# A mixture-of-experts encoder layer on one core: the router fed from sums before their norm, the last tile's gain and shift moved behind the selector

## The chip, the cores and the metric

The kernel runs on 1 core of one Trainium2 chip. The metric is the device time of that core in microseconds (us), the median of the runs shown. The core has TensorE (PE: matmuls and transposes), VectorE (DVE), ScalarE (ACT), GpSimd (POOL), and SyncE (SP), whose queue starts most transfers. The engines run their own instruction lists in order and wait for each other on semaphores.

## What is computed

One encoder layer on 512 tokens of 1024 values: an input norm, a mixer, a second norm (LayerNorm 1), then the four best of 32 experts for each token, and a last norm. The change lies between the mixer's output projection and the first expert. Cut to what matters there:

```python
mixed = hybrid_mixer(h, ...)                 # ends in y @ w_out + b_out
h = layer_norm(DN_ALPHA * h + mixed, ln1_g, ln1_b)
logits = h @ w_router + b_router             # 512 x 32
top_val, top_idx = lax.top_k(logits, 4)
gates = jax.nn.softmax(top_val, axis=-1)
# every token's row of h goes through its four experts:
#   act = min(glu, 7) * sigmoid(1.702 * glu) * (clip(lin, -7, 7) + 1),  then act @ w_exp_out[e] + b_exp_out[e]
#   weighted with its gate and summed by token
out = layer_norm(DN_ALPHA * h + ff, ln2_g, ln2_b)
```

## The kernel before

**Tiles.** The 512 tokens are four tiles of 128 rows (`x[:, i, :]`, i = 0 to 3), and a matmul covers 128 of the 1024 values at a time (k = 0 to 7). `psum` (named "banks" in the profile) has eight banks of 128x512 float32. The program has two blocks. The first (lines 411 to 1194) holds the mixer, LayerNorm 1, the router and the selection of the first expert's rows; the second (from line 1261) holds the 32 experts and the last norm. Between them all engines meet: none enters the second block before all have left the first.

**The end of the mixer.** `project(i, h, ks)` (L1092) multiplies tile i by half h of the output matrix, eight float32 matmuls of 512 columns. For each tile DVE adds the residual (L867, after four scalings at L859), takes the statistics (L869, L871), ACT takes the root (L635), and DVE normalises (L877), multiplies by the gain (L879) and adds the shift (L881). The result h1 is then used three times: SP writes it to `h1_dram`, from where later experts gather their rows; POOL scales it (L707) and SP writes it to `acc_dram`; and PE transposes it (`turn_h1`, L1128), ACT copies the transpose (`h1T`, L642; it lies in `hT`), and PE multiplies that by the router's weights `w_rt` (`route`, L1137, and one row for the bias, L1138).

**The order on PE** is written out by hand: projections, transposes and routes of neighbouring tiles interleave. After the last projection stand transpose, route and `keep_busy(n)` (L1145), which issues n products of the identity with ones that nobody reads.

**The selector.** Once the logits of all four tiles are there, DVE takes the eight largest of each row (L900), marks the four best as `hot_b` (L917), and PE counts them by expert (L1173, L1176). From the counts DVE gets `cand`, each token's place at each expert (L928), and `sel0` (L935, in `tmp`), a 0/1 matrix that picks the rows of expert 0. PE multiplies h1 by `sel0` (L1191, 32 products): this is expert 0's input, transposed. DVE then makes the gates in three bfloat16 parts (L938 to L945) and the selectors `sel_first` of the first three experts (L935 again); PE multiplies these by token numbers (L1187), and DVE turns the answer into row numbers `dst_row` (L956 to L965). At last DVE takes the low part `x_lo` of the first half of expert 0's input (L967).

**The experts.** A weight chunk of 1 MB sits in one of 12 slots of `raw`. ACT rounds it (`hi`, L1370), DVE takes the rest (`lo`, L1554), and PE makes three passes (L1789): hi by x_hi, lo by x_hi, hi by x_lo. Twelve chunks make one expert. SP loads a chunk as soon as DVE is through with the slot's last content (L1281). Before the first block ends, SP has loaded twelve chunks: eight from about 225 us on, and four once the last projection is done (L435).

## Time and profile before

| what | us |
|---|---|
| median of 3 runs | 1458.41 (1458.26 to 1458.52) |
| the profiled execution, device time | 1458.66 |
| its span, first to last instruction | 1456.9 |
| PE busy in the span | 1421.1 (98%) |
| DVE busy | 1211.8 (83%) |
| ACT busy | 971.5 (67%) |
| last projection ends | 274.1 |
| first product of the first expert | 299.6 |

A row of the trace in order of time gives the start in us, the duration in us (of several merged instructions: from the first start to the last end), the engine, the line of the kernel, the operation, output and inputs with their shapes, and the count. In brackets stands how long the engine had been idle and what ended that. A float32 matmul of the program is two records. A following matmul starts some 0.17 us before the recorded end of the one ahead of it, since matmuls are pipelined; starts are the better measure. The granted clock of TensorE is at its upper level (2.4 GHz, shown as 1.00) nearly all the time (mean 0.995); the lower level, 1.2 GHz, is shown as 0.50.

### The profile page before, as it was taken

The numbers are of one execution on the slowest core, as the hardware profiler recorded it, in microseconds if no ns is written. First come the engines' busy times: TensorE is split into PE (matmuls) and PEld (weight loads), VectorE is DVE, ScalarE is ACT, GpSimd is POOL, SyncE is SP. The second block draws the span as 40 slices with busy tenths as digits, with TensorE's granted clock in tenths as the row PEclk, the third lists the DMA queues.
The fourth block names the chain that finished last, engine by engine and source line by source line (L and its number), as shares of the span: only waits on it lengthen the run. The fifth ranks groups of instructions, "written<-read, shape, count | busy, mean of one in ns | idle before, by whom it ended". The sixth has DMA issues, their size and how long they took to land.

```text
span 1456.9 us, 20291 instructions
## 1 busy us (share of the span) xinstructions
PE 1421.1 (98%) x6459; PEld 1090.5 (75%) x6459; DVE 1211.8 (83%) x1001; ACT 971.5 (67%) x703; POOL 492.1 (34%) x307
## 2 busy tenths in 40 slices
PE   6999989999999999999999999999999999999996
PEld 3466554788888888888888888888888888888873
DVE  5533348589999999999999999999999999999985
ACT  2245660267777777777777777777777777777772
POOL 4200025143333333444444443334333343333101
PEclk9999999999999999999999999999999999999998
DMA  7220227469999999999999999999999999999943
GB/s 262 78 62 29 69 92 277 188 277 382 372 378 377 375 383 381 385 376 387 382 380 387 376 378 385 388 388 380 377 379 380 377 382 377 378 381 377 360 139 129
DMA packets 85733, 459.31 MB, mean 315 GB/s; under 512 B 11848, under 2 KB 26442, under 8 KB 36554
## 3 DMA queue, kind: packets, MB, share of 16 engines
q1 hardware_dynamic: 75190, 431.91, 75.3%
q0 software_dynamic: 9072, 24.39, 7.1%
q10 hardware_dynamic: 1444, 2.66, 0.7%
q8 instruction: 15, 0.25, 0.1%
q14 instruction: 12, 0.10, 0.0%
HBM read 443.92 MB, written 23.66 MB: 321 GB/s over the span
## 4 chain that ended last, share of the span: by engine, by line
PE 78%; DVE 1%; DVEq 0%; issue 0%; ACT 0%; ACTq 0%
PE banks L1789 72%; PE banks L1758 2%; PE banks L1764 2%; PE banks L1825 1%; PE banks L1893 0%; PE banks L1771 0%; PE banks L1898 0%; DVE raw L1723 0%; PE banks L1752 0%; DVE glu_lin L1589 0%; DVE raw L1719 0%; DVEq L1593 0%; ACT hi L1370 0%; DVE glu_lin L1595 0%; ACT raw L1454 0%
## 5 line engine op out<-in xcount | busy, mean ns | idle before, releaser
L1554 DVE TENSOR_TENSOR lo<-raw,hi 128x2048 fp32r<-128x2048 f32 x383 | 863.6, 2288 | 68.5 <-ACT hi L1370 66.7
L1370 ACT ACTIVATE hi<-raw 128x2048 fp32r<-128x2048 f32 x382 | 729.7, 1920 | 243.2 <-PE banks L1789 243.2
L1789 PE MATMUL banks<-hi,x_hi 128*128 128x512 f32 x1040 | 285.3, 396 | 2.8 <-DVE glu_lin L1589 1.5
L1789 PE MATMUL banks<-lo,x_hi 128*128 128x512 f32 x1040 | 279.0, 390 | 0.0
L1789 PE MATMUL banks<-hi,x_lo 128*128 128x512 f32 x1040 | 278.9, 389 | 0.0
L1474 POOL TENSOR_SCALAR sel<-cst,rank_e 128x128 bf16<-128x128 f32 x120 | 211.6, 1775 | 133.5 <-issue 133.5
L1789 PEld LDWEIGHTS banks<-lo,x_hi 128*128 128x128 f32 x1040 | 195.3, 188 | 41.2
L1789 PEld LDWEIGHTS banks<-hi,x_lo 128*128 128x128 f32 x1040 | 195.3, 188 | 41.1
L1789 PEld LDWEIGHTS banks<-hi,x_hi 128*128 128x128 f32 x1040 | 190.4, 188 | 39.8 <-issue 3.5
L1494 POOL DMA_INDIRECT acc_dram<-ye,dst_row x31 | 49.9, 1610 | 363.8 <-ACT ye L1391 363.8
L1789 PE MATMUL banks<-hi,a_hi 128*128 128x512 f32 x496 | 156.3, 396 | 0.0
L1789 PE MATMUL banks<-hi,a_lo 128*128 128x512 f32 x496 | 153.3, 390 | 0.0
L1789 PE MATMUL banks<-lo,a_hi 128*128 128x512 f32 x496 | 153.1, 390 | 0.0
L1789 PEld LDWEIGHTS banks<-lo,a_hi 128*128 128x128 f32 x496 | 93.1, 188 | 20.1
L1789 PEld LDWEIGHTS banks<-hi,a_lo 128*128 128x128 f32 x496 | 93.1, 188 | 19.7
L1044 PE MATMUL banks<-hT,raw 128*128 128x512 f32 x240 | 105.2, 596 | 0.0
L1789 PEld LDWEIGHTS banks<-hi,a_hi 128*128 128x128 f32 x496 | 90.8, 188 | 17.4 <-issue 0.2
L1044 PEld LDWEIGHTS banks<-hT,raw 128*128 128x128 f32 x240 | 45.5, 192 | 54.7 <-issue 53.7
L1468 POOL COPY rank_e<-rank 128x4 f32 (+1 forms) x30 | 53.7, 1790 | 91.5 <-PE banks L1752 91.5
L1485 POOL DMA_INDIRECT xg<-h_dram,dst_row x32 | 36.4, 1138 | 102.8 <-PE banks L1758 101.1
L1477 POOL COPY tok<-gate_parts 128x12 bf16 (+1 forms) x30 | 67.0, 2234 | 6.2 <-issue 5.9
L776 DVE SCALAR_TENSOR_TENSOR raw<-raw 128x1280 f32<-128x1280 f32 x4 | 6.0, 1492 | 72.1 <-ACT raw L578 72.1
(275 smaller groups left out, 1185.9 us busy)
## 6 DMA issues: line engine op xcount, KB each, us to landing
raw<-in_w_exp_in SPq DMA_DIRECT2D x256, 1024.0 KB, 7.6
raw<-in_w_exp_out SPq DMA_DIRECT2D x128, 1024.0 KB, 7.1
raw<-in_w_in SPq DMA_DIRECT2D x9, 1024.0 KB, 8.3
raw<-in_w_out SPq DMA_DIRECT2D x4, 1024.0 KB, 5.1
x<-in_x SPq DMA_DIRECT2D x4, 512.0 KB, 6.0
h_dram<-x SPq DMA_DIRECT2D x4, 512.0 KB, 3.9
bias_in<-bias_dram SPq DMA_DIRECT2D x128, 3.0 KB
raw<-acc_dram SPq DMA_DIRECT2D x4, 512.0 KB, 5.4
```

What stands on the lines that cost most here:

```text
L1044: last = pe.matmul(bank, w[:, k, P * half:P * half + P], hT[:, k, :], start=(k == 0), stop=(k == KD - 1))
L1370: act.activation(hi[:, c0 % PARTS, :], raw[:, ring_slot(c0), :], ACT.Copy).then_inc(hi_done, 1)
L1468: pool.tensor_copy(rank_e[:, :], rank[:, :, bass.ds(e, 1)].rearrange("p i a -> p (i a)"))
L1474: pool.tensor_scalar(sel[:, i, :], cst[:, C_IOTA:C_IOTA + SLOTS], rank_e[:, i:i + 1], None, ALU.is_equal)
L1477: pool.tensor_copy(tok[:, :, 6:9], gate_parts[:, :, :, bass.ds(e, 1)].rearrange("p i m a -> p i (m a)"))\
L1485: pool.indirect_dma_start(xg[:, :], None, h1_dram, bass.IndirectOffsetOnAxis(ap=dst_row[:, col:col + 1], axis=0), bounds_check=SEQ - 1, oo ...
L1494: pool.indirect_dma_start(acc_dram, bass.IndirectOffsetOnAxis(ap=dst_row[:, col:col + 1], axis=0), ye[:, :], None, compute_op=ALU.add).the ...
L1554: dve.tensor_tensor(lo[:, c0 % PARTS, :], raw[:, ring_slot(c0), :], w_hi.bitcast(F32), ALU.subtract).then_inc(lo_done, 1)
L1758: last = pe.transpose(psum[:, 6 + k // 4, P * (k % 4):P * (k % 4) + P], xg[:, P * k:P * k + P], ident)
L1764: last = pe.transpose(psum[:, 6 + k // 4, P * (k % 4):P * (k % 4) + P], lin[:, P * k:P * k + P], ident)
L1789: last = pe.matmul(psum[:, bank + n, :], s[:, k, :], w[:, at:at + 512], start=(first and m == 0 and new), stop=(closes and m == steps - 1 ...
L1825: last = pe.matmul(psum[:, n, :], one_row[r, :], bias_in[r, :], start=False, stop=True)
```

## The change

The router's input is no longer h1. With s the sum before LayerNorm 1, m and r its mean and reciprocal deviation, the logits are r * (s @ (gain * w)) - r * m * sum(gain * w) + sum(shift * w) + bias, and the kernel computes them so:

- DVE folds the gain into `w_rt` once, early (at the step `z`, 0), and makes the two column sums; PE adds them over the partitions and adds the bias (3 small products after tile 0's projection), and DVE keeps the two rows as `off_e`.
- `turn_sum(i)` transposes the sums, in two halves of four, each as soon as that half has been added; `route` loses its bias row. DVE may overwrite the sums (normalise) only when they have been transposed. For each tile DVE makes `shift_e` (two small operations), and at the end four `scalar_tensor_tensor` that give the logits.
- The projections of tiles 1 to 3 are cut into halves with transposes and routes between them; the route of tile 2 stands in the middle of the last half.
- The gain and shift of the last tile run on DVE behind `sel0`. PE first multiplies the selector by tiles 0 to 2 for four k, then waits for the last tile.
- What DVE did behind LayerNorm 1 (first chunk's `lo`, constants) becomes `prepare()`, ahead of tile 2's second half.
- `x_lo` of the first half moves ahead of `sel_first`; the products of `sel_first` go to the end of PE's list in the first block; `dst_row` is computed in the second block, on DVE, before the third chunk's `lo`, and POOL's first gather waits for it.
- `keep_busy` goes from 4 + 4 + 13 + 6 to 2 + 8 + 4 products.
- SP leaves the first block without waiting for the last tile's write to `acc_dram`; POOL waits for it in the second block, and DVE before the fifth chunk.
- Some buffers lie elsewhere in SBUF, and `channel_params` grows by 16 columns.

The core of the diff:

```diff
-                    sp.dma_start(acc_dram[P * i:P * i + P, :], scaled[i]).then_inc(acc_out, 16)
-                sp.dma_start(acc_dram[SEQ:SEQ + P, :], scaled_pad).then_inc(acc_out, 16)
+                    if i == NT - 1:
+                        sp.dma_start(acc_dram[P * i:P * i + P, :], scaled[i]).then_inc(acc_last, 16)
+                    else:
+                        sp.dma_start(acc_dram[P * i:P * i + P, :], scaled[i]).then_inc(acc_out, 16)
+                    if i == 0:
+                        sp.dma_start(acc_dram[SEQ:SEQ + P, :], scaled_pad).then_inc(acc_out, 16)
...
+                sp.wait_ge(acc_out, 16 * NT)
...
+                for i in range(NT):
+                    if i < NT - 1:
+                        std1(i)
+                    for h in range(2):
+                        act.wait_ge(h1T_ready, 2 * i + h + 1)
+                        act.activation(h1T[:, 4 * h:4 * h + 4, P * (i % 2):P * (i % 2) + P],
+                                       psum[:, 4 + h, :].rearrange("p (k s) -> p k s", k=4), ACT.Copy).then_inc(h1T_copied, 1)
...
+                    if i == NT - 1:
+                        std1(i)
...
                     if what == "z":
+                        if n == 0:
+                            dve.wait_ge(rt_in, 32)
+                            dve.wait_ge(param_in, 16)
+                            dve.tensor_tensor(by_shift, w_rt[:, :, :],
+                                              vec[:, V_LN1B:V_LN1B + KD].unsqueeze(2).broadcast_to([P, KD, E]), ALU.mult)
+                            dve.drain()
+                            dve.tensor_tensor(w_rt[:, :, :], w_rt[:, :, :],
+                                              vec[:, V_LN1G:V_LN1G + KD].unsqueeze(2).broadcast_to([P, KD, E]), ALU.mult)
+                            dve.tensor_reduce(wsum[:, E:2 * E], by_shift.rearrange("p k e -> p e k"), AX.X, ALU.add)
+                            dve.drain()
+                            dve.tensor_reduce(wsum[:, 0:E], w_rt[:, :, :].rearrange("p k e -> p e k"), AX.X,
+                                              ALU.add).then_inc(rt_folded, 1)
                         dve.wait_ge(z_logs, n + 1)
...
+                dve.wait_ge(rt_sums, 1)
+                dve.tensor_scalar(off_e[:, 0, :], psum[:, 7, 0:E], -1.0, None, ALU.mult)
+                dve.tensor_copy(off_e[:, 1, :], psum[:, 7, E:2 * E])
                 dve.drain()
...
+                def gain_shift(i):
+                    dve.tensor_tensor(x[:, i, :], x[:, i, :], gain_b, ALU.mult)
+                    dve.drain()
+                    dve.tensor_tensor(x[:, i, :], x[:, i, :], shift_b, ALU.add).then_inc(h1_ready, 1)
+
+                def prepare():
+
+                    dve.wait_ge(table_out, 16 * 3)
+                    dve.wait_ge(hi_done, 1)
+                    dve.tensor_tensor(lo0[:, :], raw[:, ring_slot(0), :], hi0[:, :].bitcast(F32),
+                                      ALU.subtract).then_inc(lo_done, 1)
...
                     for n in range(2):
+                        if (i, n) == (NT - 2, 1):
+                            prepare()
...
+                    dve.tensor_scalar(shift_e[:, i, :], off_e[:, 0, :], mv[:, i, 0:1], rstd[:, i:i + 1], ALU.mult, ALU.mult)
+                    dve.drain()
+                    dve.tensor_tensor(shift_e[:, i, :], shift_e[:, i, :], off_e[:, 1, :], ALU.add)
+                    dve.wait_ge(h1T_ready, 2 * (i + 1))
                     dve.tensor_scalar(x[:, i, :], x[:, i, :], mv[:, i, 0:1], rstd[:, i:i + 1], ALU.subtract, ALU.mult)
                     dve.drain()
-                    dve.tensor_tensor(x[:, i, :], x[:, i, :], gain_b, ALU.mult)
-                    dve.drain()
-                    dve.tensor_tensor(x[:, i, :], x[:, i, :], shift_b, ALU.add).then_inc(h1_ready, 1)
...
+                    if i < NT - 1:
+                        gain_shift(i)
+
+                dve.wait_ge(rt_ready, 1)
+                for i in range(NT):
+                    dve.scalar_tensor_tensor(logit[:, i, :], psum[:, 6, E * i:E * i + E], rstd[:, i:i + 1], shift_e[:, i, :],
+                                             ALU.mult, ALU.add)
...
                 for i in range(NT):
                     dve.max(top[:, i, :], logit[:, i, :])
...
                 occupants(sel0, 0).then_inc(sel0_ready, 1)
+                gain_shift(NT - 1)
                 dve.tensor_tensor(gate[:, :, :], left[:, :, :], gsum[:, :].unsqueeze(2).broadcast_to([P, NT, E]), ALU.mult)
...
+                dve.wait_ge(x0_half_hi, 1)
+                dve.tensor_tensor(x0_lo[:, 0:4, :], psum[:, 0:4, 0:SLOTS],
+                                  x0_hi[:, 0:4, :].bitcast(F32), ALU.subtract).then_inc(x0_half_lo, 1)
...
                 last.then_inc(sel_first_ready, 1)
...
-                dve.wait_ge(first_picked, 1)
...
+                def turn_sum(i):
                     for h in range(2):
-                        project(i, h, IN_ORDER_K)
-
-                def turn_h1(i):
-                    pe.wait_ge(h1_ready, i + 1)
-                    if i:
-                        pe.wait_ge(h1T_copied, i)
-                    for k in range(KD):
-                        last = pe.transpose(psum[:, 4 + k // 4, P * (k % 4):P * (k % 4) + P], x[:, i, P * k:P * k + P], ident)
-                    last.then_inc(h1T_ready, 1)
+                        pe.wait_ge(out_added, 2 * i + h + 1)
+                        if i:
+                            pe.wait_ge(h1T_copied, 2 * i + h - 1)
+                        for k in range(4):
+                            last = pe.transpose(psum[:, 4 + h, P * k:P * k + P], x[:, i, P * (4 * h + k):P * (4 * h + k) + P], ident)
+                        last.then_inc(h1T_ready, 1)
...
-                    pe.wait_ge(h1T_copied, i + 1)
-                    pe.wait_ge(rt_in, 32)
                     o = psum[:, 6, E * i:E * i + E]
                     for k in range(KD):
-                        pe.matmul(o, h1T[:, k, P * i:P * i + P], w_rt[:, k, :], start=(k == 0), stop=False)
-                    last = pe.matmul(o, ones[0:1, :], b_rt[:, :], start=False, stop=True)
+                        if k % 4 == 0:
+                            pe.wait_ge(h1T_copied, 2 * i + k // 4 + 1)
+                        last = pe.matmul(o, h1T[:, k, P * (i % 2):P * (i % 2) + P], w_rt[:, k, :], start=(k == 0),
+                                         stop=(k == KD - 1))
...
-                project_all(1)
-                turn_h1(0)
-                project_all(2)
+                pe.wait_ge(rt_folded, 1)
+                pe.wait_ge(av_copied, 2)
+                pe.matmul(psum[:, 7, 0:E], ones, wsum[:, 0:E], start=True, stop=True)
+                pe.matmul(psum[:, 7, E:2 * E], ones, wsum[:, E:2 * E], start=True, stop=False)
+                pe.matmul(psum[:, 7, E:2 * E], ones[0:1, :], b_rt[:, :], start=False, stop=True).then_inc(rt_sums, 1)
+                project(1, 0, IN_ORDER_K)
+                turn_sum(0)
+                project(1, 1, IN_ORDER_K)
+                pe.wait_ge(out_added, 2)
+                project(2, 0, IN_ORDER_K)
                 route(0)
-                turn_h1(1)
-                project_all(3)
+                turn_sum(1)
+                project(2, 1, IN_ORDER_K)
+                pe.wait_ge(out_added, 4)
+                project(3, 0, IN_ORDER_K)
                 route(1)
-                turn_h1(2)
-                pe.wait_ge(out_added, 2 * NT)
-                keep_busy(4)
+                turn_sum(2)
+                project(3, 1, IN_ORDER_K[:4])
                 route(2)
-                turn_h1(3)
-                keep_busy(4)
+                project(3, 1, IN_ORDER_K[4:])
+                turn_sum(3)
+                keep_busy(2)
                 route(3)
-                keep_busy(13)
+                keep_busy(8)
...
-                keep_busy(6)
+                keep_busy(4)
...
+                pe.wait_ge(h1_ready, NT - 1)
+
+                def rows_of_first(o, k, tiles):
+                    for i in tiles:
+                        last = pe.matmul(o, x[:, i, P * k:P * k + P], sel0[:, i, :], start=(i == 0), stop=(i == NT - 1))
+                    return last
+
+                for k in range(4):
+                    rows_of_first(psum[:, k, 0:P], k, range(NT - 1))
+                pe.wait_ge(h1_ready, NT)
+                for k in range(4):
+                    last = rows_of_first(psum[:, k, 0:P], k, [NT - 1])
+                last.then_inc(x0_half_ready, 1)
+                for k in range(4, KD):
+                    last = rows_of_first(psum[:, 7, P * (k - 4):P * (k - 4) + P], k, range(NT))
+                last.then_inc(xT_ready, 1)
+                pe.wait_ge(sel_first_ready, 1)
...
                 pool.memset(bias_in[0:64, :], 0.0)
                 pool.drain()
...
+                pool.wait_ge(rows_set, 1)
...
+                def first_rows():
+
+                    dve.wait_ge(first_picked, 1)
+                    dve.tensor_reduce(got_first[:, :, :], psum[:, 4, 0:FIRST * PICKED].rearrange("p (g a b) -> p g a b", a=3, b=3),
+                                      AX.X, ALU.add)
+                    dve.drain()
+                    dve.tensor_scalar(row_first[:, :], got_first[:, :, 1], cst[:, C_NEG_DUMP:C_NEG_DUMP + 1],
+                                      cst[:, C_DUMP:C_DUMP + 1], ALU.mult, ALU.add)
+                    dve.drain()
+                    dve.tensor_tensor(slot[:, 0:FIRST, 0], row_first[:, :], got_first[:, :, 0], ALU.add)
+                    dve.tensor_copy(slot[:, 0:FIRST, 1], got_first[:, :, 2])
+                    dve.drain()
+                    dve.tensor_copy(dst_row[:, :], slot[:, :, 0]).then_inc(rows_set, 1)
+
                 def over_count():
 
...
                                   x0_hi[:, 4:KD, :].bitcast(F32), ALU.subtract).then_inc(x_lo_done, 1)
...
+                    if q == PARTS:
+                        dve.wait_ge(acc_last, 16)
                     part(0, q)
```

**PE, the projections of tiles 1 to 3.** L1092 (L1127 after) is a projection, L1128 (L1157) transposes, L1137 and L1138 (L1166) route. Before, from the last matmuls of tile 0 on:

```order
L1092 MATMUL banks<-raw,y 128x512 x30
L1128 MATMUL banks<-cst,x 128x128 x8
L1092 MATMUL banks<-raw,y 128x512 x16
L1137 MATMUL banks<-w_rt,hT 128x32 x8
L1138 MATMUL banks<-b_rt,cst 128x32
L1128 MATMUL banks<-cst,x 128x128 x8
L1092 MATMUL banks<-raw,y 128x512 x16
L1137 MATMUL banks<-w_rt,hT 128x32 x8
L1138 MATMUL banks<-b_rt,cst 128x32
L1128 MATMUL banks<-cst,x 128x128 x8
L1145 MATMUL banks<-cst 128x128 x4
L1137 MATMUL banks<-w_rt,hT 128x32 x8
```

After, from the first half of tile 1 on (ahead of it stand the three small products):

```order
L1127 MATMUL banks<-raw,y 128x512 x8
L1157 MATMUL banks<-cst,x 128x128 x8
L1127 MATMUL banks<-raw,y 128x512 x16
L1166 MATMUL banks<-w_rt,hT 128x32 x8
L1157 MATMUL banks<-cst,x 128x128 x8
L1127 MATMUL banks<-raw,y 128x512 x16
L1166 MATMUL banks<-w_rt,hT 128x32 x8
L1157 MATMUL banks<-cst,x 128x128 x8
L1127 MATMUL banks<-raw,y 128x512 x4
L1166 MATMUL banks<-w_rt,hT 128x32 x8
L1127 MATMUL banks<-raw,y 128x512 x4
L1157 MATMUL banks<-cst,x 128x128 x8
```

Two routes and one set of transposes that stood behind the last projection now stand ahead of its last matmul.

**DVE, behind the count.** `tmp` is `sel0`. Before:

```order
L928 SCALAR_TENSOR_TENSOR cand<-banks,hot_b 128x128
L935 SCALAR_TENSOR_TENSOR tmp<-cst,cand 128x512
L938 TENSOR_TENSOR gate<-left,gsum 128x128
L942 CAST gate_parts<-gate 128x4x32
L945 TENSOR_TENSOR left<-gate,gate_parts 128x128
```

After:

```order
L974 SCALAR_TENSOR_TENSOR cand<-banks,hot_b 128x128
L981 SCALAR_TENSOR_TENSOR tmp<-cst,cand 128x512
L892 TENSOR_TENSOR x<-x,affine 128x1024
L894 TENSOR_TENSOR x<-x,affine 128x1024
L985 TENSOR_TENSOR gate<-left,gsum 128x128
L989 CAST gate_parts<-gate 128x4x32
L992 TENSOR_TENSOR left<-gate,gate_parts 128x128
```

The last tile's gain and shift have moved in between `sel0` and the gates.

**DVE, the start of the second block.** Before:

```order
L1554 TENSOR_TENSOR lo<-raw,hi 128x2048
L1611 TENSOR_TENSOR x_lo<-banks,x_hi 128x512
L1554 TENSOR_TENSOR lo<-raw,hi 128x2048 x5
```

After:

```order
L1602 TENSOR_TENSOR lo<-raw,hi 128x2048
L1673 TENSOR_TENSOR x_lo<-banks,x_hi 128x512
L1648 TENSOR_REDUCE got_first<-banks 128x9
L1651 TENSOR_SCALAR row_first<-got_first,cst 128x3
L1654 TENSOR_TENSOR slot<-row_first,got_first 128x3
L1655 COPY slot<-got_first 128x3
L1657 CAST dst_row<-slot 128x4
L1602 TENSOR_TENSOR lo<-raw,hi 128x2048 x5
```

Five small operations now stand ahead of the third chunk's `lo`.

## Rows read from the trace of the kernel before

**Rows 1.** Busy time in a stretch of the expert loop: start:end, length, engines, clock, DMA.

```profile
400.00:1400.00 1000.00, 1000.00 (x4771) 816.78 (x4770) 927.46 (x651) 756.89 (x454) 380.17 (x218) 1.00 0.99 379
```

**Rows 2.** PE in order of time, projections to the first product of the second block.

```profile
242.50 1.04 PE L1128 MATMUL banks<-cst,x 128*128 128x128 f32 x8
...
257.11 1.87 PE L1137 MATMUL banks<-w_rt,hT 128*128 128x32 f32 x16
258.90 0.40 PE L1138 MATMUL banks<-b_rt,cst 1*128 1x32 f32 x2
259.24 1.09 PE L1128 MATMUL banks<-cst,x 128*128 128x128 f32 x8
260.17 13.90 PE L1092 MATMUL banks<-raw,y 128*128 128x512 f32 x32
273.90 1.87 PE L1137 MATMUL banks<-w_rt,hT 128*128 128x32 f32 x16
...
284.92 4.79 PE L1145 MATMUL banks<-cst 128*128 128x128 f32 x26
...
291.33 4.63 PE L1191 MATMUL banks<-tmp,x 128*128 128x128 f32 x40
...
299.61 1.16 PE L1789 MATMUL banks<-hi,x_hi 128*128 128x512 f32 x4
...
305.17 1.07 PE L1789 MATMUL banks<-hi,x_hi 128*128 128x512 f32 x4
```

**Rows 3.** DVE in order of time, the mixer and LayerNorm 1.

```profile
91.27 1.49 DVE L776 SCALAR_TENSOR_TENSOR raw<-raw 128x1280 f32<-128x1280 f32 x1 [33.62 <-ACT raw L578]
...
234.94 0.69 DVE L867 TENSOR_TENSOR x<-x,banks 128x512 f32<-128x512 f32 x1
...
276.60 0.81 DVE L877 TENSOR_SCALAR x<-x,mv,rstd 128x1024 f32<-128x1024 f32 x1
...
278.79 1.23 DVE L881 TENSOR_TENSOR x<-x,affine 128x1024 f32<-128x1024 f32 x1
```

**Rows 4.** DVE in order of time, the selector.

```profile
285.03 0.49 DVE L900 MAX8 top<-banks 128x8 f32<-128x32 f32 x4 [1.13 <-PE banks L1138]
...
287.80 0.29 DVE L917 TENSOR_TENSOR hot_b<-above,level 128x128 bf16<-128x128 f32 x1
...
290.09 0.29 DVE L928 SCALAR_TENSOR_TENSOR cand<-banks,hot_b 128x128 f32<-128x128 f32 x1 [0.66 <-PE banks L1176]
...
291.07 0.28 DVE L938 TENSOR_TENSOR gate<-left,gsum 128x128 f32<-128x128 f32 x1
...
295.12 0.22 DVE L951 TENSOR_SCALAR rank<-cand 128x128 f32<-128x128 f32 x1
```

**Rows 5.** ACT in order of time: a copy of 512 columns.

```profile
295.10 0.60 ACT L653 ACTIVATE x_hi<-banks 128x512 fp32r<-128x512 f32 x1 [5.16 <-PE banks L1191]
```

**Rows 6.** POOL in order of time, the scaling of the last tile.

```profile
280.10 2.77 POOL L707 TENSOR_SCALAR vpad<-x 128x1024 f32<-128x1024 f32 x1 [14.03 <-DVE x L881]
```

**Rows 7.** DVE in order of time, the same moment.

```profile
280.08 0.16 DVE L886 CAST strict_b<-cst 128x128 bf16<-128x128 f32 x1
280.16 1.06 DVE L887 CAST ones_b<-cst 128x128 bf16<-128x128 f32 x1
```

**Rows 8.** DVE in order of time, row numbers and the second block's start.

```profile
296.28 0.19 DVE L956 TENSOR_REDUCE got_first<-banks 128x9 f32<-128x27 f32 x1 [0.80 <-PE banks L1187]
...
297.30 0.68 DVE L967 TENSOR_TENSOR x_lo<-banks,x_hi 128x512 fp32r<-128x512 f32 x1
...
302.16 2.28 DVE L1554 TENSOR_TENSOR lo<-raw,hi 128x2048 fp32r<-128x2048 f32 x1
```

**Rows 9.** Two stretches of 1 us, columns as in rows 1.

```profile
286.00:287.00 1.00, 1.00 (x6) 1.00 (x6) 0.90 (x4) 0.66 (x2) 0.00 (x0) 0.50 0.82 291
...
289.00:290.00 1.00, 1.00 (x20) 0.99 (x20) 0.36 (x2) 0.94 (x1) 0.00 (x0) 0.86 1.02 418
```

**Rows 10.** Transfers issued from 270 to 300 us: count, size, us to landing.

```profile
h_dram<-x SPq DMA_DIRECT2D x1, 512.0 KB, 8.9
```

131 lines of the change are left out of this document (52 added, 79 removed).

## Prediction, made before the changed kernel was run

> **What bounds the kernel now.** I read the busy time by stretches first: in the expert loop PE is busy all of the time [rows 1], and no wait stands ahead of it. The change leaves the loop alone, so its length stays, and what counts is when it starts: the first product of the first expert, at 299.61 [rows 2]. The second view is each engine's timeline from the last projection to that product, 25.7 us from 273.90 to 299.61 [rows 2]. Follow the longest chain there: add, statistics, normalise, gain, shift, transpose, copy, route; at 285.03 DVE starts to look for the best four [rows 4]; from `cand` at 290.09 comes `sel0`, and from 291.33 PE is busy with expert 0's rows until the first block ends [rows 2, 4]. Whatever the change takes out of this chain moves the 1100 us behind it as a whole.
>
> **1. The last projection comes later.** Work that stood behind it now stands ahead of it. Starts in [rows 2] price it: a route's eight products 258.90 - 257.11 = 1.79, its bias row 259.24 - 258.90 = 0.34, a set of transposes 260.17 - 259.24 = 0.93, a tile's projection 273.90 - 260.17 = 13.73. Ahead of the last projection now come two more routes (3.58), one more set of transposes (0.93), two products of 32 columns and a bias row (2 x 0.22 + 0.34 = 0.78), less one bias row (0.34): 4.95. One wait is new. Before, tile 0's projection ended at 242.50 - 13.73 = 228.77, long before DVE came to add it at 234.94 [rows 2, 3]; the old order had a whole tile to hide this, the new one half. PE is through with half of tile 1 at 228.77 + 0.78 + 6.87 = 236.4 and with the first four transposes at 236.9. DVE first has two small reads for `off_e`, about 0.35 by small rows such as the 0.22 at 295.12 [rows 4], then add, statistics, add, each taken at 0.69 [rows 3]: the second half is there at 237.4. PE waits 0.55 (0 to 1.1, if the adds shift by half a us either way). Sum: **5.5 later, 279.4 instead of 273.90.**
>
> **2. From there to the selector.** The last half is added by 280.3 (0.2 for the matmul to end, 0.69), its four transposes end at 281.0, ACT copies them in 0.60 [rows 5] until 281.6. PE is meanwhile through with two dummy products and the first half of the route, and ends the route at about 281.4 + 1.79 + 0.2 = 283.4. The norm's own chain runs beside it: the root comes behind ACT's copies now (281.9), then reciprocal, two operations for `shift_e`, 0.81 for the normalising [rows 3], also about 283.4. Four operations for the logits take about what the four searches take, 0.49 [rows 4]: the search starts at 284.0 against 285.03, **1.0 earlier**. What leaves the path is gain and shift, 2 x 1.23 [rows 3], and most of one engine-to-engine round.
>
> **3. The search.** DVE had waited 0.66 for the count, since 26 records of dummy products (284.92 + 4.79 = 289.7) kept PE beyond `hot_b` (287.80 + 0.29) [rows 2, 4]. After, 8 dummies take some 1.8 (row products of the same 128 columns take 0.223 each, step 4) and end near 285.3, while `hot_b` comes at 287.1; the count then needs at most half a us, and DVE is ready only at 284.0 + (290.09 - 0.66 - 285.03) = 288.4. So `cand` and `sel0` come **1.65 earlier**.
>
> **4. Gain and shift behind `sel0`.** They cost DVE 2.46. PE meanwhile does 12 of its 32 row products. 20 of these take (4.63 - 0.17) us [rows 2], so 0.223 each, 12 take 2.7: this hides the two, with 0.2 to spare. It costs DVE all the same: from the gates (291.07) to the last of `sel_first` (295.12) [rows 4] nothing gets shorter, `x_lo` adds 0.6 [rows 8] and a short wait for ACT's half. `sel_first` is ready at 295.2 - 1.65 + 2.46 + 0.75 = 296.8; PE is through with the rows, which before ended at 299.0 (their last group starts at 296.1) with 0.3 of `sel_first` products among them, at 299.0 - 1.65 - 0.3 = 297.05. No wait yet, but 0.25 of cover is all there is.
>
> **5. POOL beside DVE.** The last tile's scaling (2.77) starts 0.1 after the shift, so now beside the gates' casts. Before, it started at 280.10, and of two casts of one shape the one at 280.08 took 0.16 and the one at 280.16 took 1.06 [rows 6, 7]: 0.9 for a cast that met POOL. I take one such hit (bounds: 0, and all of the 2.77). DVE is then ready at 297.7, PE waits 0.65, and the block ends 1.0 earlier instead of 1.65. The Trainium skill (SBUF — State Buffer, "Who interferes with whom") says that GpSimd and such DVE operations share a port pair, and that the holder keeps it for its whole instruction; by that the cast would have ended at 282.87, and the trace had it end at 281.22. By the rule the sum would be rival B.
>
> **6. The second block.** `dst_row` costs 297.30 - 296.28 = 1.02 [rows 8] and stands ahead of the third chunk's `lo`, which ran 302.16 to 304.44 for a product that started at 305.17 [rows 2, 8]: cover 0.73. It will end at 305.5 on the old scale, so PE waits **0.4** once; a chunk is 2.28 on DVE against 2.72 on PE, and the delay is made good within three chunks.
>
> **7. At no cost.** The folding of gain into `w_rt` stands where DVE idles 33.62 [rows 3]. `prepare()` runs while PE projects; tile 2's second half is transposed 5 us later. SP's first loads in the loop start behind `acc_last`, issued near 295 and landed near 299, no later than POOL began before; twelve chunks are loaded ahead by then.
>
> **Sum:** 1.65 - 0.65 + (-0.4) = 0.6 earlier. Of the profiled execution's 1458.66 that is 1458.06; the median lies 0.25 below that execution, so **1457.8**. Own range: without POOL's hit and with no wait at the third chunk 1456.8; with 0.5 more wait in step 1, 1458.3.
>
> **Rival A, the clock falls into the row products (slower).** The granted clock went to 0.50 at 285.9 and came back at 289.3 [rows 9], after 12 us of transposes, routes and dummies. It fell on dummies and cost nothing but their length. The new order has fewer dummies and 1.7 us in which PE waits for `hot_b`, then a wait for `sel0`; a similar fall that comes 3 to 4 us later lies over the row products, which at 1.2 GHz take twice as long. 3.4 us of it cost 1.7: 1459.5; two in a row 1461.2. It decides against the change from 1.2 us of overlap on. Against it speaks that the low stretch is shorter now, 10 us from 279.4 with full projections right ahead. The Trainium skill (TensorE: Matmul & The Clock Gate, "What's actually happening") ties the clock to how busy PE has been; the records show PE busy 1.00 when it fell, so they can't say which way this goes. Chance 0.22.
>
> **Rival B, POOL blocks DVE for its whole 2.77.** `sel_first` comes at 296.8 + 2.6 = 299.4, the block ends 0.85 later than before instead of earlier, with the 0.4 it is 1459.7. For it: nothing in [rows 7] shows the two-input operations that stand there now. Chance 0.08.
>
> **Rival C, the write of the last tile holds the barrier.** SP leaves the first block only when the last tile has landed in `h1_dram`; it is now issued at 292.1. Before it took 8.9 [rows 10], with four chunk loads in the queue; that would be 301.0, 2.0 later than the block ended before, with the 0.4 of step 6 1460.8. Against it: the loads start at 279.6 and are 4.2 MB, over by 291 at the rate of rows 9's stretch. Chance 0.05.
>
> **Rival D, it gains more.** If the wait in step 1 is nil, no cast is hit and the third chunk is covered, 1.65 + 0.55 = 2.2: 1456.2. Each alone is plausible, all three not. Chance 0.08. That the change doesn't do what it says (PE held up by DVE's order in the projections, so that the last one comes still later) is in the forecast's upper end and 0.02 beyond it.
>
> **How the numbers follow.** Forecast 0.55, A 0.22, B 0.08, C 0.05, D 0.08, beyond 0.02. The range reaches from 1456.2 to 1460.2: the forecast, B, D and the single fall of A. A measurement of this kernel can tell 0.2%, 2.9 us, from no change: faster means under 1455.5, slower above 1461.3. The first needs more than D, some gain that I don't see (0.05); the second needs A twice with a little more, or C and A together (0.06); within it lies 0.89.
>
> **What would show it.** After: last projection over at 279.4; the search (MAX) at 284.0; `cand` at 288.4 with no wait for PE; the first expert's first product at 298.6; one wait of PE of 0.4 for `lo` at the third chunk; casts of `gate_parts` once at about 1 us instead of 0.23; clock 1.00 from 290 on. The forecast is wrong if the first product starts outside 297.4 to 300.5, or if the loop's length changes at all.

## The result, and the profile after

| | median, us | lowest to highest | executions |
|---|---|---|---|
| kernel before | 1458.38 | 1458.12 to 1458.91 | 10 |
| changed kernel | 1463.11 | 1460.62 to 1465.46 | 10 |

The ratio is 1.0029, 95% interval 1.0020 to 1.0037: **slower by 4.7 us**, or 0.3%. The prediction (1457.8, range 1456.2 to 1460.2) was wrong in sign and in size. The profiled execution took 1463.83 with a span of 1462.1, 5.2 more than before. The spread is a finding too: in these ten executions the kernel before keeps within 0.8 us, and the changed one varies by 4.8. (In the 84 further executions of the kernel before that ran beside the experiments, four lie at 1460.3 to 1460.6 and all others between 1458.0 and 1459.6.)

The two traces side by side show where the 5.2 came from. All are starts on PE, in the execution profiled of each kernel.

| moment | before | after | later by | of it new |
|---|---|---|---|---|
| mixer, projection of tile 0 | 216.75 | 218.76 | 2.01 | +2.01 |
| first product of expert 0 [rows 2] | 299.61 | 300.39 | 0.78 | -1.23 |
| its third chunk [rows 2] | 305.17 | 306.50 | 1.33 | +0.55 |
| its bias rows | 322.47 | 323.92 | 1.45 | +0.12 |
| expert 31's bias rows, behind the loop | 1402.76 | 1405.30 | 2.54 | +1.09 |
| gate products at the end of the experts | 1428.19 | 1433.37 | 5.18 | +2.64 |

Only the second and the third line are places that the prediction spoke of, and there it was close. The first, the fifth and the last line add up to 5.7, and PE has no new instruction there. The first piece is in the mixer. PE in order of time, before (lines L1009 and L1077) and after (L1044 and L1112): the same products, the same wait in front of them.

```profile
208.84 1.95 PE L1009 MATMUL banks<-raw,cst 128*128 128x512 f32 x4 [2.28 <-ACT raw L625]
210.63 2.32 PE L1077 MATMUL banks<-raw,vpad 128*128 128x512 f32 x8
```

```profile
209.15 2.49 PE L1044 MATMUL banks<-raw,cst 128*128 128x512 f32 x4 [2.29 <-ACT raw L636]
211.43 3.53 PE L1112 MATMUL banks<-raw,vpad 128*128 128x512 f32 x8
```

They take 2.28 and 3.36 from start to start instead of 1.79 and 2.16: 1.7 of the 2.01 (the other 0.3 is there when the wait begins to end, 209.15 against 208.84). The stretches of the changed kernel say why: start:end, length, busy time of PE, its weight loads, DVE, ACT and POOL, the granted clock, the transfers.

```profile
210.50:213.80 3.30, 3.30 (x6) 1.37 (x5) 1.86 (x2) 0.69 (x1) 0.00 (x0) 0.50 0.00 0
289.00:292.30 3.30, 3.06 (x26) 3.07 (x27) 2.94 (x7) 2.01 (x3) 0.00 (x0) 0.50 1.01 422
326.50:329.90 3.40, 3.40 (x10) 2.63 (x9) 3.40 (x3) 0.70 (x1) 0.00 (x0) 0.50 1.00 417
```

Three times the clock is at its lower level, 1.2 GHz; before it was so once, on unread products [rows 9]. (The last 9 to 11 us are low in both kernels and are left out here.) Each of the three follows on a wait of PE: 2.29 for `raw` (above), 2.61 for `hot_b`, 1.58 for `glu_lin`. PE of the changed kernel in order of time, where [rows 2] showed the kernel before:

```profile
281.00 0.60 PE L1157 MATMUL banks<-cst,x 128*128 128x128 f32 x4
281.95 0.66 PE L1157 MATMUL banks<-cst,x 128*128 128x128 f32 x4 [0.34 <-DVE x L921]
...
284.60 2.03 PE L1174 MATMUL banks<-cst 128*128 128x128 f32 x16
289.24 0.21 PE L1211 MATMUL banks<-hot_b,strict_b 128*128 128x32 bf16 x1 [2.61 <-DVE hot_b L963]
...
289.63 2.05 PE L1174 MATMUL banks<-cst 128*128 128x128 f32 x8
291.48 7.73 PE L1223 MATMUL banks<-tmp,x 128*128 128x128 f32 x64
299.35 0.46 PE L1239 MATMUL banks<-tok_first,sel_first 128*128 128x9 bf16 x12
...
306.50 1.16 PE L1854 MATMUL banks<-hi,x_hi 128*128 128x512 f32 x4 [0.40 <-DVE lo L1602]
...
325.89 1.54 PE L1854 MATMUL banks<-hi,x_hi 128*128 128x512 f32 x4 [1.58 <-DVE glu_lin L1637]
```

The last piece is at the end of the experts. The chain of work that ended last, before the gate products:

```profile
1424.99 5.89 PE banks L1854 x26
1430.88 2.48 issue
1433.37 2.00 PE banks L1836 x12
```

"Issue" is time in which PE waits for nothing that the profile's views show. The trace's instruction records show what stands there: a branch. Behind the experts PE's program reads a count and then has `with pe.If(more > 0):` around a block for tokens that find no room at their expert. No product of that block ran, so the branch jumps over it. Its record in the changed kernel starts at 1427.53 and lasts 5.57; in the kernel before it starts at 1424.91 and lasts 0.47. PE still has products in line when the branch starts, until 1430.88 here; of the 5.57 they cover 3.35.

The queues' packets fit. Code comes on two queues of kind "instruction", in packets of 16 KB on q8 and mostly 8 KB on q14. q8 is PE's: waits added to PE's program alone (e1_after_pad below) move its first packet from 38.2 to 26.7 and leave that of q14 at 27.7. The first line is the kernel before in 1419:1425, the second the changed kernel in 1430:1434; in its stretch 1419:1430 there is no such packet.

```profile
q8 instruction: 1, 0.02, 1.4%
```

```profile
q8 instruction: 2, 0.03, 3.2%
```

Before, the packet starts at 1419.8, 5.1 ahead of the branch. In the changed kernel the first of the two starts at 1430.7, 3.1 behind the start of the branch, and PE is back at 1433.37. Read together: the branch waits until a page of code has come, and in the kernel before that page was already there.

The change takes 14 unread or bias products out of PE's program and adds a few waits. A float32 product is four instructions, two matmuls and two weight loads (the traces have 6459 of each before and 6431 after), so the program becomes 55 instructions shorter ahead of the loop, and every page behind begins at another product.

In the loop between, PE is busy all of the time, as before [rows 1]:

```profile
400.00:1400.00 1000.00, 1000.00 (x4774) 817.05 (x4773) 927.93 (x652) 758.08 (x455) 375.17 (x219) 1.00 0.99 379
```

### The profile page after: what moved, and what is told of

Read it like the earlier page. It is cut to its first block, busy times and chain, and to the rows that moved or that the text cites. A ratio compares the mean times of both kernels' runs of the same rounds, so it can differ in the third digit from the quotient of the medians.

```text
span 1462.1 us, 20266 instructions
## 1 busy us (share of the span) xinstructions
PE 1419.9 (97%) x6431; PEld 1087.8 (74%) x6431; DVE 1216.6 (83%) x1019; ACT 971.9 (66%) x707; POOL 484.5 (33%) x307
## 4 chain that ended last, share of the span: by engine, by line
PE 77%; DVE 2%; issue 1%; DVEq 0%; ACT 0%; ACTq 0%
PE banks L1854 71%; PE banks L1823 2%; PE banks L1829 2%; DVE lo L1602 1%; PE banks L1890 1%; PE banks L1958 0%; PE banks L1836 0%; PE banks L1963 0%; DVE raw L1788 0%; PE banks L1817 0%; DVE raw L1784 0%; DVE glu_lin L1637 0%; DVEq L1641 0%; ACT hi L1416 0%; DVE glu_lin L1643 0%
## 5 line engine op out<-in xcount | busy, mean ns | idle before, releaser
L1520 POOL TENSOR_SCALAR sel<-cst,rank_e 128x128 bf16<-128x128 f32 x120 | 205.8, 1729 | 139.3 <-issue 139.3
```

The costliest lines, as they stand in the source:

```text
L1520: pool.tensor_scalar(sel[:, i, :], cst[:, C_IOTA:C_IOTA + SLOTS], rank_e[:, i:i + 1], None, ALU.is_equal)
```

## The experiments

In all of them the kernel before ran on the same chip beside them. **Theory P (pages):** the standstill near 1430 (PE idle, "issue") comes from where PE's pages of code begin, and is worth 2.5 to 3. **Theory C (clock):** falls of the granted clock behind waits of PE cost the rest, and they come or stay away by execution. **Theory N (new order):** the new order itself brought the loss, by its transfers or its semaphores.

### Only the place of the pages: e1_after_pad, e2_before_shift, e5_before_cut

The changed kernel with 110 waits on a semaphore that is long set, two to an instruction, at the head of PE's program: 55 instructions (its trace has 55 more of them on PE).

```diff
             def _(pe):
+                for _ in range(110):
+                    pe.wait_ge(first_set, 1)
                 pe.wait_ge(cst_in, 16)
```

> The changed kernel with 110 waits on a semaphore that is long up (some 55 instructions) put ahead of PE's first work, where PE has nothing to do for 9.6 us. Theory code loading: the 2.5 us that PE stands idle near 1431, ahead of the last norm's products, is the fetch of a code page behind a jump; the change took some 55 instructions out of PE's list and so moved the page borders; with them back the gap is gone, the time is 2.5 us less than the changed kernel's, and a 16 KB fetch stands near 1420 again. Rival: the gap is a transfer or a semaphore that comes late; then it stays at 2.5 us, and so does the time.

Measured: 1458.97 (1458.32 to 1460.78), before 1458.75, ratio 1.0002 (0.9993 to 1.0012). Nothing but 55 instructions without effect took 4.1 us off, against N, and more than the 2.5 that the expectation gave to the standstill. PE has no standstill at the end, the branch takes 0.35, and a packet of code comes at 1419.4 again. (A wait of 1.36 to 1.39 on "issue", some 11 us ahead of the gate products, is in every kernel of this document and changes nothing between them.) In this execution the clock fell neither in the mixer nor behind `glu_lin`, but fully over the row products, which take 8.92 instead of 7.41 in traces without a fall. From the count to the first product of expert 0 it is 11.78 instead of 11.16 (e3_filled), so 0.6 of these 1.5 are lost: the rest lies in a wait of 0.76 for `sel_first` that PE has otherwise.

```profile
287.63 0.19 PE L1213 MATMUL banks<-hot_b,strict_b 128*128 128x32 bf16 x1 [2.61 <-DVE hot_b L963]
...
289.56 8.92 PE L1225 MATMUL banks<-tmp,x 128*128 128x128 f32 x64 [0.43 <-DVE tmp L981]
```

The other way round, the kernel before moved by 201 instructions, which the expectation takes for 55 short of a page:

```diff
             def _(pe):
+                for _ in range(402):
+                    pe.wait_ge(first_set, 1)
                 pe.wait_ge(cst_in, 16)
```

> The kernel before with 402 such waits (some 201 instructions, which is 55 less than a 16 KB page of 256 holds), so that the page borders lie against PE's later work as in the changed kernel, and nothing else differs. Theory code loading: PE stands idle for 2.5 us ahead of the last norm's products and the kernel takes 1460.9 instead of 1458.4. Rival: no gap, 1458.4. If the waits last beyond 9.6 us, PE's first transposes show it and that is taken off.

Measured: 1474.36 (1473.38 to 1475.72), ratio 1.0110 (1.0095 to 1.0126). The standstill is there, and the trace has 16 of the 16 KB packets instead of 15; but the run is a poor test: the waits themselves held PE until 22.88, and the mixer ended 9.4 late. With 3.35 for the standstill and 2.7 for a fall of the clock around it (1439.1 to 1445.9) that makes 15.4 of the 15.6.

```profile
22.88 5.18 PE L978 MATMUL banks<-cst,x 128*128 128x128 f32 x32 [22.88 <-issue]
...
1440.33 2.10 PE L1773 MATMUL banks<-b_out,gateT 32*128 32x512 f32 x6 [3.35 <-issue]
```

A cleaner one shortens the old program instead, by unread products alone:

```diff
                 pe.wait_ge(out_added, 2 * NT)
-                keep_busy(4)
                 route(2)
                 turn_h1(3)
-                keep_busy(4)
                 route(3)
                 keep_busy(13)
...
-                keep_busy(6)
                 pe.wait_ge(sel0_ready, 1)
```

> The kernel before without 14 of its 27 unread products (those ahead of route 2, ahead of route 3 and behind the rank sums; the 13 ahead of the count stay). PE's program gets 56 instructions shorter, nearly as much as by the change (55), and the order of its work stays the old one. If the 2.5 us at the end of the loop comes from where PE's pages of code begin, PE stands again at the first transposes of the last but one expert's tail, the fetch near 1420 is missing, the clock falls behind the wait, and the time is 1458.7 + 2.5 + 0.8 = 1462.0 (1461.2 without the fall). If the wait belongs to the new order (its transfers, its semaphores), it is absent and the time stays at 1458.7. Apart from that, fewer unread products may bring a fall of the clock over the projections or the row products: up to 1.7 more.

Measured: 1469.18 (1468.39 to 1470.04), before 1458.71, ratio 1.0071 (1.0058 to 1.0085). The standstill is there, in the old order, with the branch at 6.04 and the packets of code at 1404.3 and 1433.6 and none between. That decides for P against N.

```profile
1429.99 3.40 PE banks L1786 x15
1433.39 2.97 issue
1436.35 2.23 PE banks L1768 x12
```

The run took 7.2 more than expected, and most of that is the clock: 13.65 us at the lower level from 280.9 on, over the last routes and transposes and the unread products behind them, and another fall right behind the standstill. The first product of expert 0 started at 304.72, 5.1 late (5.0 against e4_before_again, which like this trace has a fall in the mixer). Behind the standstill, the products up to the last gate products take 11.74 instead of 10.08, so that fall costs 1.7.

```profile
281.00:294.50 13.50, 12.39 (x55) 11.73 (x55) 7.19 (x25) 5.90 (x6) 2.77 (x1) 0.50 0.75 293
1438.10:1441.30 3.20, 3.20 (x7) 1.24 (x5) 0.00 (x0) 0.00 (x0) 0.00 (x0) 0.50 0.00 0
```

The 14 unread products had been worth 5 us there; they were not idle ballast.

### The kernel before again: e4_before_again

The same file, to see how much two traces of one program differ.

> The kernel before once more, for its trace. Theory clock: whether a low stretch becomes a fall hangs on when it comes; the kernel before shows one fall, near 286, on unread products, at 1458.4. If a second trace shows it at the same place, the places are set by the kernel and not by chance; if it shows others, the time should differ by 1 to 2 us.

Measured: 1458.8, span 1457.1. The clock fell in the mixer this time and not on the selector's unread products:

```profile
209.00:212.00 3.00, 3.00 (x5) 1.35 (x4) 1.13 (x3) 0.69 (x1) 0.00 (x0) 0.50 0.00 0
```

PE reached that place 0.8 earlier than in the first trace (208.02 against 208.84) and left it 0.87 later (217.62 against 216.75). Yet the first product of expert 0 is only 0.08 later (299.69): from the search to `cand` it is 4.33 here and was 5.06 in the first trace, where the fall on the unread products held back the count. So the place of a fall is not the program's alone. The mixer's fall was a risk of the kernel before as well; the changed kernel's trace happened to have it and the trace of before did not.

### Waits filled with unread products: e3_filled, e6_after_filled, e7_before_filled

The changed kernel, with unread products where PE waits longest ahead of work that counts, and 54 waits at the head to bring the pages back to their old place.

```diff
+                for _ in range(54):
+                    pe.wait_ge(first_set, 1)
                 pe.wait_ge(cst_in, 16)
...
                         tiles = GROUPS[g][1]
+                        if g == 1:
+                            for _ in range(2):
+                                pe.matmul(psum[:, 4, :], ident, cst[:, 0:512], start=True, stop=True)
                         pe.wait_ge(y_sq, normed_by(g))
...
                 keep_busy(8)
+                for _ in range(2):
+                    pe.matmul(psum[:, 0, :], ident, cst[:, 0:512], start=True, stop=True)
...
+                        if isinstance(v, int) and v == 1:
+                            pe.wait_ge(gateT_copied, 1)
+                            for n in (512, P, P):
+                                pe.matmul(psum[:, 5, 0:n], ident, cst[:, 0:n], start=True, stop=True)
                         pe.wait_ge(lin_ready, v)
```

> The changed kernel with unread products in the three places where its trace showed the clock fall or a wait ahead of a fall: 2 of 512 columns ahead of the second group's norm sum (PE waits 2.3 us there), 2 of 512 columns behind keep_busy(8) (PE waits 2.6 us for hot_b), one of 512 and two of 128 columns ahead of expert 1's first product (PE waits 1.6 us), and as many waits at the start as bring the code pages back. Theory clock: no fall before the end, the runs lie within 1 us, and the time is the kernel before less what the new order gains (1.9 in the row products' start) plus 0.55 at the third chunk and 0.3 in the mixer: 1457.3. Rival, the new order costs time of its own: above 1459 with the clock at 1.00.

Measured: 1457.75 (1457.18 to 1458.37), before 1458.75, ratio 0.9993 (0.9984 to 1.0002). e6_after_filled is the same without the 54 waits, 27 instructions shorter:

> The changed kernel with the unread products of e3_filled in three places (2 x 512 columns in the mixer, 2 x 512 ahead of the count, 512 + 128 + 128 ahead of the second expert) and without the waits at the start. PE's program is 28 instructions longer than the changed kernel's, 27 shorter than e3_filled's. Theory: falls of the clock cost the changed kernel 1.7 (mixer), about 0.8 (rows) and 1.1 (loop) where they come, and the wait for code 2.5. With the fillers the falls are gone: 1460.3 if the wait for code is still there, 1457.8 if 28 instructions are enough to move it away; all executions within 1 us of each other. Rival, the wait for code alone made all of the difference (e1_after_pad got rid of 4.1 with little done to the clock): the fillers bring nothing, and the time is 1462.5 to 1463 with the wait, with a spread of 4 us as in the changed kernel.

Measured: 1457.35 (1456.97 to 1458.39), before 1458.71, ratio 0.9991 (0.9982 to 1.0000). No fall of the clock in either trace ahead of PE's last products, a mean clock of 0.996 to 0.997 in all 22 executions, and a spread of 1.2 and 1.4. Against e1_after_pad that is 1.6 less (1.2 for e3_filled): what the falls cost when the pages are right. The page's place is not delicate: 27 instructions more than the changed kernel's were enough.

e7_before_filled puts the same fillers into the kernel before, in the mixer and ahead of the second expert, and takes 5 of the 6 unread products behind the count out, so that the program keeps its length.

> The kernel before with the fillers of e3_filled in the mixer and ahead of the second expert, and 5 of its 6 unread products behind the rank sums taken out, so that PE's program is as long as before. This prices the new order alone, by comparison with e3_filled (1457.75). Theory: the clock falls in the mixer or on the unread products of the selector, by turns, and costs the kernel before 0 to 0.9; filled it takes 1458.4, and the new order is worth 0.6 as forecast. Rival, the new order is worth nothing and e3_filled's lead over the kernel before is its fillers' alone: this one takes 1457.7.

Measured: 1458.26 (1458.01 to 1460.28), before 1458.71, ratio 0.9998 (0.9989 to 1.0007). On the same chip e6_after_filled took 1457.35: **the new order is worth 0.9**; 0.6 had been forecast. The intervals of the two ratios overlap, but only 2 of the 11 executions of e6_after_filled lie above the lowest of e7_before_filled. The clock is not quite out of this figure: in e7_before_filled it still fell on the 13 unread products ahead of the count (285.0 to 288.5), and DVE waited 0.66 for the count. But the 20 executions of the kernel before beside the experiments with a mean clock of 0.997, so without a fall ahead of the end, have a median of 1458.36, and e6_after_filled lies 1.0 below that too.

### The pages, all else filled: e10_filled_same_pages, e11_after_again

e6_after_filled with the same unread columns in fewer, wider products, so that PE's program is as long as the changed kernel's again.

```diff
-                keep_busy(8)
-                for _ in range(2):
+                for _ in range(4):
                     pe.matmul(psum[:, 0, :], ident, cst[:, 0:512], start=True, stop=True)
...
-                keep_busy(4)
+                keep_busy(3)
                 pe.wait_ge(sel0_ready, 1)
```

> e6_after_filled (1457.35) with the same unread columns in fewer products: the 8 unread products of 128 columns ahead of the count become 2 of 512, and of the 4 behind the count one is left out. PE's program is 28 instructions shorter than e6_after_filled's and as long as the changed kernel's, to one instruction; as much unread work (but for 0.2 us), the same order, the same fillers. If the start of PE's pages of code makes the wait at the end of the loop, it is back: the fetch near 1420 is missing and PE stands 2.5 to 3.0 us at the first transposes or bias products after 1428; 1457.35 + 2.5 = 1459.9, up to 1460.7 with a fall of the clock behind it. If the wait belongs to something else in the changed kernel (the clock, the transfers), it stays away: 1457.4.

Measured: 1461.97 (1459.87 to 1464.78), before 1458.57, ratio 1.0025 (1.0016 to 1.0034).

```profile
1426.53 0.61 PE L1858 MATMUL banks<-hi,x_lo 128*128 128x512 f32 x2
1430.12 2.01 PE L1840 MATMUL banks<-b_out,gateT 32*128 32x512 f32 x12 [2.98 <-issue]
```

28 instructions fewer than e6_after_filled bring the standstill back, 2.98, and the branch takes 6.07 instead of 0.47. The profiled execution took 1460.62, 3.3 more than e6_after_filled's median. The median is 4.6 more. The further 1.3 goes roughly with the clock: the four executions of 1459.9 to 1461.4 have a mean clock of 0.995 to 0.997, the five up to 1463.6 one of 0.995 or 0.996, the two above 1463.9 one of 0.992 and 0.994. A fall behind the standstill is likely, since e5_before_cut and the next kernel show one there, but no trace of a long execution of this kernel was taken. The changed kernel once more, without any edit:

> The changed kernel once more, on the chip of the others here. Theory: the wait for code of 2.5 is in every execution, the falls of the clock are not: the fastest execution is 1457.35 + 2.5 + one fall of 0.5 to 1.1 = 1460.6 as before, the slowest has three falls (mixer 1.7, rows 0.8, loop 1.1) and lies near 1464. The granted clock over the whole span goes with the time: 0.996 in the fast ones, 0.992 in the slow ones. Rival, the difference of 4.7 was the chip's or the hour's: it is under 2 here.

Measured: 1463.29 (1461.53 to 1465.8), ratio 1.0034 (1.0021 to 1.0046): not the chip's and not the hour's doing. Its falls lie over the row products and behind the standstill (2.94 here), none in the mixer and none in the loop. The fall behind the standstill costs 1.6: from the first gate products to the last it is 11.71, where the traces without such a fall have 10.04 to 10.08.

```profile
290.00:293.00 3.00, 3.00 (x15) 3.00 (x16) 2.85 (x4) 0.00 (x0) 0.75 (x1) 0.50 0.47 194
1433.30:1436.50 3.20, 3.20 (x8) 1.51 (x5) 0.00 (x0) 0.00 (x0) 0.00 (x0) 0.50 0.00 0
```

```profile
1431.36 2.03 PE L1836 MATMUL banks<-b_out,gateT 32*128 32x512 f32 x12 [2.94 <-issue]
...
1443.07 1.98 PE L1836 MATMUL banks<-b_out,gateT 32*128 32x512 f32 x4
```

### What the new order left on the table: e8_act_rows, e9_act_order, e12_count_later

Two small waits remained: 0.76 for `sel_first`, behind casts that POOL slows, and 0.40 at the third chunk. e8_act_rows takes e3_filled and moves the last tile's scaling to ACT, and `first_rows()` two chunks back.

```diff
+                act.wait_ge(h1_ready, NT)
+                act.activation(scaled[NT - 1], x[:, NT - 1, :], ACT.Copy, scale=ALPHA_DN).then_inc(last_scaled, 1)
                 act.wait_ge(x0_half_ready, 1)
...
-                for i in range(NT):
+                for i in range(NT - 1):
                     pool.wait_ge(h1_ready, i + 1)
...
-                first_rows()
                 for q in range(2, IN_CHUNKS + AHEAD - 1):
+                    if q == 4:
+                        first_rows()
```

> e3_filled with the last tile's scaling by 1024 columns on ACT instead of POOL (ACT stands idle from 289.4 to 293.4 there) and first_rows() behind the fourth chunk's lo instead of ahead of the third's. Theory: the casts of gate_parts take 0.23 each instead of 0.93 and 0.62, sel_first is ready 1.1 earlier and PE's 0.76 of wait for it is gone, and so is the 0.40 at the third chunk: 1457.75 - 0.76 - 0.40 = 1456.6. Rival, the casts were slow for another reason than POOL: 1457.35. Rival, the rows of the first experts come too late for the gather (its transposes began 315.9 in e3_filled): slower than 1457.75.

Measured: 1460.13 (1458.53 to 1462.35), before 1458.71, ratio 1.0012 (1.0003 to 1.0021). The theory held and the rival on the gather too. DVE's three casts beside POOL's scaling, in the changed kernel, and then with the scaling on ACT:

```profile
293.83 0.93 DVE L989 CAST gate_parts<-gate 128x128 bf16<-128x128 f32 x1
...
295.20 0.23 DVE L989 CAST gate_parts<-left 128x128 bf16<-128x128 f32 x1
...
295.87 0.62 DVE L989 CAST gate_parts<-left 128x128 bf16<-128x128 f32 x1
```

```profile
291.96 0.23 DVE L992 CAST gate_parts<-gate 128x128 bf16<-128x128 f32 x1
...
292.63 0.23 DVE L992 CAST gate_parts<-left 128x128 bf16<-128x128 f32 x1
...
293.30 0.23 DVE L992 CAST gate_parts<-left 128x128 bf16<-128x128 f32 x1
```

The wait for `sel_first` went, the second block began at 297.38 instead of 298.50. But the row numbers came later, the gather with them, and PE stood 2.70 for its landing. The executions vary by 3.8, and those from 1458.5 to 1461.5 have the same mean clock (0.995 or 0.996), so that spread is not the clock's; whether it is the gather's landing no trace shows.

```profile
316.92 1.09 PE L1834 MATMUL banks<-cst,xg 128*128 128x128 f32 x8 [2.70 <-DMA xg<-h_dram,dst_row]
```

e9_act_order keeps `first_rows()` where it was and moves the subtraction for the second half of `x0_lo` behind the third chunk's `lo` instead (on e6_after_filled, with the scaling on ACT).

> e6_after_filled (1457.35) with the last tile's scaling on ACT instead of POOL, as in e8_act_rows (the first expert's first product came 1.1 earlier there), and with the subtraction for the second half of x0_lo (0.68 us, wanted by the fifth chunk only) behind the third chunk's lo instead of ahead of it; first_rows() stays ahead of it, so the gather is not held up. Theory: the casts take 0.23, PE's wait of 0.76 for sel_first and the 0.40 for the third chunk's lo are gone, and the gather lands in time for the transposes: 1457.35 - 1.16 = 1456.2. Rival, the gather still holds PE (in e8_act_rows it did, for 2.7): 1456.6 to 1458.

Measured: 1457.37 (1456.54 to 1458.62), before 1458.57, ratio 0.9991 (0.9982 to 1.0000). Nothing gained on e6_after_filled. From the start of the row products to the second block it is 8.08 instead of 8.96, 0.88 saved. It was given back on DVE, which from there on works without a gap: one small operation of `first_rows()` started earlier, met POOL's setting of `xg` and took 0.99 instead of 0.40, and DVE's `x_lo` for the second expert started 0.64 later (321.59 against 320.95, blocks beginning at the same 297.97).

```profile
300.43 0.99 DVE L1659 TENSOR_SCALAR row_first<-got_first,cst 128x3 f32<-128x3 f32 x1
```

```profile
300.45 0.96 POOL L1560 MEMSET xg<- 128x1024 f32 x1
```

The small operation ends at 301.42 and POOL's at 301.41. In e6_after_filled the same two end at 301.43 and 301.41, so the earlier start brought nothing.

So DVE bounds the first expert, not PE. e12_count_later takes 1.3 us of work that nobody wants there out of DVE's way (it ran on another chip than e9_act_order, with the kernel before beside it at 1458.47):

```diff
                     part(0, q)
-                    if q == TURN_AT:
-                        over_count()
                 x_part(1)
                 clip(0)
                 swiglu(0)
                 part(0, IN_CHUNKS + AHEAD - 1)
+                over_count()
```

> e9_act_order (1457.37) with over_count(), 1.3 us of small operations on DVE, taken from the middle of the first expert's chunks and put behind the fourth chunk of the second expert's supply. In e9_act_order the selector ended 0.88 sooner after the start of the row products than in e6_after_filled, but DVE works without a gap from there to the second expert and had its x_lo and glu_lin 0.6 later, so that the second expert's first product came no earlier. Theory: DVE is what gave the gain back; with 1.3 us less ahead of it, its glu_lin is ready 1.2 us sooner after the first expert's first product, PE's wait ahead of the second expert is gone, and the time is 1457.37 - 0.6 = 1456.8. Rival, what gave it back is the place where DVE is hit by POOL or the bias products that glu_lin waits for: no change, 1457.4.

Measured: **1456.51** (1455.85 to 1457.33), before 1458.47, ratio 0.9986 (0.9977 to 0.9995), the fastest of all: 2.0 below the kernel before, 6.6 below the changed one's median. DVE now has a gap and waits for PE's bias rows:

```profile
321.14 1.23 DVE L1645 TENSOR_SCALAR glu_lin<-banks 128x1024 f32<-128x1024 f32 x1 [0.84 <-PE banks L1902]
```

The 0.41 at the third chunk is still there in this trace (the same small operation meets POOL's setting of `xg`, 0.99 again); it was not tried further.

## Why the prediction was wrong, and where it was right

**The step that failed** is in the first paragraph: "The change leaves the loop alone, so its length stays, and what counts is when it starts." The work in the loop did stay as it was. But what lies between the second expert's start and the end depends on two things that an edit ahead of it moves: where PE's pages of code begin (2.5 to 3.0 us of standstill at 1430, in a branch that waits for code), and whether the clock falls behind a wait (1.1 in the loop of the profiled execution, 1.6 behind the standstill in e11_after_again). Of the 5.2 in the traces 0.8 was there when the first expert began, where 1.0 less had been forecast and 2.0 had come from the mixer, and 4.4 came behind it. The prediction itself named this condition, a loop whose length changes, as one that makes it wrong; it gave it no chance and no place in the range. The sum lacked a term for the 55 instructions less, although the diff shows the products that are gone, and one for a fall of the clock in the mixer (1.7).

On the 2.01 that were there before the new order begins: 0.3 came with DVE, which stood 0.43 on "issue" just ahead (at 174.15); 1.7 is the fall of the clock. That DVE's own pages are the cause of the 0.3 was not tried.

Taking 2.01 off the starts, the steps came out so:

- **Step 1**, last projection at 279.4: 281.00 - 2.01 = 278.99. The wait of 0.55 for the added half was about 0.2.
- **Step 2**, search at 284.0: 286.12 - 2.01 = 284.11. Right to 0.1, although the four logits took 0.97 instead of 0.49.
- **Step 3**, `cand` at 288.4: 290.09 - 2.01 = 288.08, 0.3 better. PE, as said, was not waited for any more; but it stood 2.61 ahead of `hot_b`, where 1.7 had been put down. The reason given was wrong in part: e4_before_again has the same 26 records of unread products and no wait of DVE for the count, since the clock did not fall on them there. The 0.66 was the price of that fall, which by Rival A "cost nothing but their length".
- **Step 5**, one cast slowed to about 1: 0.93, and a second one to 0.62. With the clock up, PE's wait was 0.76 (e3_filled) where 0.65 had been said. The rule of the Trainium skill (SBUF — State Buffer, "Who interferes with whom"), by which POOL's whole 2.77 would have blocked DVE, doesn't hold for these casts either: the one that began 0.19 after POOL's operation ended at 294.76, with POOL's ending at 296.41. The 128x3 operation of `first_rows()` did wait until POOL's had ended (e9_act_order).

```profile
293.64 2.77 POOL L721 TENSOR_SCALAR vpad<-x 128x1024 f32<-128x1024 f32 x1 [14.82 <-DVE x L894]
```

- **First product** at 298.6: 300.39 - 2.01 = 298.38. The fall over the count and the rows cost nothing here: from the count to the first product it is 11.15, and 11.16 in e3_filled without a fall.
- **Step 6**, 0.4 at the third chunk: 0.40. That it would be made good was wrong as to who pays: DVE, not PE, is behind in the first expert, and the bias rows kept all of it (1.45 late against 1.33).
- **Steps 4 and 7**: the gain and shift were hidden, and no loss shows at `acc_last` or the folding.
- **The sum**: 0.6 forecast for the new order; 0.9 measured (e6_after_filled against e7_before_filled).

**Rival A** came in the selector, but not at its price: the clock fell over the count or the row products in all three traces of this order without fillers. It cost nothing in the profiled execution, 0.6 in e1_after_pad and 0.7 in e11_after_again, where A had said 1.7, since PE's wait for `sel_first` took up the rest. What A lacked is that the clock falls behind other pauses of PE as well: in the mixer (1.7), ahead of the second expert (1.1), behind the standstill (1.6). The Trainium skill (TensorE: Matmul & The Clock Gate, "What's actually happening") says that the phase in which the clock is judged runs free of the program; the traces of one program with its fall in the mixer once and in the selector once agree. A's chance of 0.22 can't be judged by the time, which the standstill set; that the change would end above 1461.3 had been given 0.06. **Rivals B, C and D** did not come.

The 4.7 between the medians come apart by four kernels of the new order, with and without fillers, at either place of the pages:

| | pages as in the changed kernel | moved by 27 to 55 instructions |
|---|---|---|
| without fillers | 1463.11 (again: 1463.29) | 1458.97 (e1_after_pad) |
| with fillers | 1461.97 (e10_filled_same_pages) | 1457.35 (e6_after_filled), 1457.75 (e3_filled) |

The pages are worth 4.1 or 4.6, the fillers 1.1 or 1.6. From e7_before_filled (1458.26), then: -0.9 for the new order, +4.6 for the pages, +1.1 for falls of the clock that fillers prevent: 1463.11. (The kernel before lies 0.1 above e7_before_filled, so 4.7 is left of the 4.8.) Of the part of the pages 2.5 to 3.0 are the standstill, read from four traces (a fifth, e2_before_shift, has 3.35). The rest, 1.1 to 2.1, is not seen in every trace: a fall behind the standstill costs 1.6 where it comes (e11_after_again, 1.7 in e5_before_cut), and the profiled executions of the changed kernel and of e10_filled_same_pages have none. That the long executions owe their length to such falls rests on their mean clock (0.992 or 0.993 in the three above 1464.5, 0.996 in those under 1461.5) and not on a trace of each.
